# A one-core decoder step: six entries moved in the hand-written order of the recurrence, and one new wait

## What is computed

```
def step(S, inp):
    r_t, w_t, k_t, v_t, kk_t, a_t = inp
    sa = einsum("bhvk,bhk->bhv", S, -kk_t)
    S = S * w_t + sa[..., None] * (kk_t * a_t) + v_t[..., None] * k_t
    o_t = einsum("bhvk,bhk->bhv", S, r_t)
    return S, o_t
...
o = (o - mean) * rsqrt(var + LNX_EPS) * lnx_g + lnx_b
o = o + sum(r * k * r_k) * v
o = o * silu(g)
```

## Time and profile before

| what | value |
|---|---|
| median of three runs | 1921.43 us (1921.3 to 1922.53) |
| the profiled execution | 1924.37 us, span 1922.6 us |
| TensorE busy | 1791.9 us (93%) |
| VectorE busy | 1035.1 us (54%) |
| ScalarE busy | 824.5 us (43%) |
| GpSimd busy | 262.1 us (14%) |
| mean granted TensorE clock | 0.981 |

### The profile page before, as it was taken

One profiled execution on the slowest core, in us unless ns is written; L12 is line 12 of the kernel. 1 busy time (PEld: TensorE's weight loads), 2 busy tenths in 40 slices (PEclk: granted clock), 3 DMA queues, 4 the chain that ended last, 5 costly groups with the idle time before them and its releaser, 6 DMA issues.

```text
span 1922.6 us, 44084 instructions
## 1 busy us (share of the span) xinstructions
PE 1791.9 (93%) x18432; PEld 1521.4 (79%) x18432; DVE 1035.1 (54%) x1654; ACT 824.5 (43%) x1555; POOL 262.1 (14%) x331
## 2 busy tenths in 40 slices
PE   7999999999999999999999999999999998777897
PEld 6988999999888887799987676767776775333697
DVE  6744354463588888245445443444464444676334
ACT  4334233333588887424233332323334444655233
POOL 0300000000256665232000000000000000010132
PEclk9999999999999999999999999999999998999899
DMA  7534544554345653244799999999999999999441
GB/s 280 194 136 171 179 161 166 180 167 160 110 125 153 157 129 96 98 166 166 309 343 420 419 421 396 415 426 426 425 426 404 423 423 375 420 390 363 189 144 71
DMA packets 155929, 510.45 MB, mean 266 GB/s; under 512 B 60289, under 2 KB 82178, under 8 KB 110978
## 3 DMA queue, kind: packets, MB, share of 16 engines
q1 hardware_dynamic: 153442, 503.66, 69.1%
q10 hardware_dynamic: 2304, 4.20, 0.8%
HBM read 472.86 MB, written 32.32 MB: 263 GB/s over the span
## 4 chain that ended last, share of the span: by engine, by line
PE 35%; DMA 15%; DVE 3%; ACT 2%; issue 2%; SPq 1%; DVEq 0%; ACTq 0%
DMA at_vraw<-in_cache_v 15%; PE psP L2673 8%; PE psP L2674 8%; PE psP L2675 8%; PE at_psO L2727 5%; PE at_psS L2706 4%; SPq L2086 0%; PE psP L2772 0%; PE at_psT L2718 0%; SPq L2126 0%; ACT at_p_w L2393 0%; ACT at_p_w L2391 0%; PE psP L2794 0%; DVE at_o_new L2590 0%; DVE at_p_rc L2618 0%
## 5 line engine op out<-in xcount | busy, mean ns | idle before, releaser
L2673 PE MATMUL psP<-xhi,whi 128*128 128x320 f32 x1488 | 475.7, 320 | 2.9 <-DVE xlo L2560 1.9
L2675 PE MATMUL psP<-xhi,wlo 128*128 128x320 f32 x1488 | 460.9, 310 | 0.0
L2674 PE MATMUL psP<-xlo,whi 128*128 128x320 f32 x1488 | 460.6, 310 | 0.0
L2673 PEld LDWEIGHTS psP<-xhi,whi 128*128 128x128 f32 x1488 | 280.5, 188 | 66.7 <-issue 65.2
L2435 DVE TENSOR_TENSOR wlo<-wraw,whi 128x2048 fp32r<-128x2048 f32 x92 | 212.9, 2315 | 204.6 <-ACT whi L2261 204.4
L2261 ACT ACTIVATE whi<-wraw 128x2048 fp32r<-128x2048 f32 x92 | 176.0, 1913 | 278.0 <-PE psP L2675 276.7
L2674 PEld LDWEIGHTS psP<-xlo,whi 128*128 128x128 f32 x1488 | 281.0, 189 | 0.1
L2675 PEld LDWEIGHTS psP<-xhi,wlo 128*128 128x128 f32 x1488 | 280.4, 188 | 0.0
L139 PE MATMUL psP<-xhi,whi 128*128 128x320 f32 x704 | 218.1, 310 | 2.6 <-DVE wlo L174 2.3
L140 PE MATMUL psP<-xlo,whi 128*128 128x320 f32 x704 | 217.5, 309 | 0.0
L141 PE MATMUL psP<-xhi,wlo 128*128 128x320 f32 x704 | 217.5, 309 | 0.0
(11 more groups left out here) (382 smaller groups left out, 3080.0 us busy)
## 6 DMA issues: line engine op xcount, KB each, us to landing
wraw<-in_weights SPq DMA_DIRECT2D x156, 1024.0 KB, 5.9
at_kraw<-in_cache_k SPq DMA_DIRECT2D x96, 1024.0 KB, 10.9
at_vraw<-in_cache_v SPq DMA_DIRECT2D x94, 1024.0 KB, 10.7
at_kraw<-in_cache_k SPq DMA_DIRECT2D x64, 512.0 KB, 9.4
at_vraw<-in_cache_v SPq DMA_DIRECT2D x62, 512.0 KB, 10.6
rw_s0t<-in_s0T SPq DMA_DIRECT2D x16, 256.0 KB, 3.5
o_wkv_s<-rw_SN SPq DMA_DIRECT2D x16, 256.0 KB, 3.4
wraw<-in_weights ACTq DMA_DIRECT2D x16, 256.0 KB, 3.7
```

Of the source, the lines that this page charges most:

```text
L2673: pe.matmul(out, wh, c_.xhi[:, kc, :], start=(kc == 0), stop=False)
L2674: pe.matmul(out, wh, c_.xlo[:, kc, :], start=False, stop=False)
L2675: last = pe.matmul(out, wl, c_.xhi[:, kc, :], start=False, stop=(kc == NM - 1))
```

## The change

Six entries of ORDER get another place, none is added or dropped. On ScalarE, Ht goes ahead of Pc and Q4 ahead of A12. On GpSimd, Vnx goes ahead of Rz. On VectorE, Bz goes from behind Z1 to ahead of it, directly behind ST2, and bonus from ahead of Z1 to behind it. The entry of y moves back in the string, behind O0, which changes its place towards none of GpSimd's other steps; SP's place for the load of g moves with it. And y gets a wait: in slot s it now waits until VectorE has done Bz of the same slot (tile t + 3). The order of TensorE's steps and of SP's transfers is the same as before.

```diff
@@ ORDER
-P.t.s4 F.a.sq P.t.Ht F.v.cs P.t.AB F.a.kk0 P.v.s3 F.a.Pc R.t.U0 P.v.D4s R.t.mean P.v.D P.a.Ht F.a.ka1 P.v.Dt P.t.XB
-R.a.U0 R.v.cen P.t.D2 F.g.k2 P.a.XB P.v.FR R.a.csq R.t.SA0 R.t.Q4 P.g.ID P.v.KK R.a.SA0 P.a.D2 P.a.A12 F.g.csm R.t.S0
-R.a.Q4 R.t.var R.v.ST0 R.t.U4 P.v.D2t R.a.SP1 R.t.U1 R.a.lnv F.v.rk F.t.ss P.t.W R.a.U1 R.a.U4 R.a.rstd P.v.Kt R.t.SA1
+P.t.s4 F.a.sq P.t.Ht F.v.cs P.t.AB F.a.kk0 P.v.s3 P.a.Ht F.a.Pc R.t.U0 P.v.D4s R.t.mean P.v.D F.a.ka1 P.v.Dt P.t.XB
+R.a.U0 R.v.cen P.t.D2 F.g.k2 P.a.XB P.v.FR R.a.csq R.t.SA0 R.t.Q4 P.g.ID P.v.KK R.a.SA0 P.a.D2 R.a.Q4 P.a.A12 F.g.csm
+R.t.S0 R.t.var R.v.ST0 R.t.U4 P.v.D2t R.a.SP1 R.t.U1 R.a.lnv F.v.rk F.t.ss P.t.W R.a.U1 R.a.U4 R.a.rstd P.v.Kt R.t.SA1
 P.t.D4t R.a.SA1 F.v.ssm P.a.Kn R.t.SA4 P.v.W R.t.S1 P.a.D4t R.t.O1 R.a.SA4 R.v.ST1 R.v.on P.t.Y R.g.SAx R.a.O1 F.a.ln
-P.v.Bt R.t.U2 F.g.Rz P.v.Y R.t.O4 F.a.rn F.t.bon R.a.U2 P.v.Yt F.a.Pm R.g.Vnx F.v.kk R.t.SA2 R.a.O4 P.t.E R.a.SA2
-F.v.Az R.a.ong R.t.SN P.a.E R.g.oy F.a.Pi P.v.Et R.a.SP2 R.t.S2 P.a.Bn R.v.SNa F.g.ka P.t.E2t R.v.ST2 P.t.Z1 F.v.bonus
-R.g.y R.a.SP3 R.t.U3 P.a.E2t P.v.Z1 R.t.O0 R.a.U3 R.t.O2 F.v.Bz R.a.O0 F.g.Kz R.t.SA3 R.a.xh P.t.X R.a.SA3 R.a.O2
+P.v.Bt R.t.U2 R.g.Vnx F.g.Rz P.v.Y R.t.O4 F.a.rn F.t.bon R.a.U2 P.v.Yt F.a.Pm F.v.kk R.t.SA2 R.a.O4 P.t.E R.a.SA2
+F.v.Az R.a.ong R.t.SN P.a.E R.g.oy F.a.Pi P.v.Et R.a.SP2 R.t.S2 P.a.Bn R.v.SNa F.g.ka P.t.E2t R.v.ST2 F.v.Bz P.t.Z1
+R.a.SP3 R.t.U3 P.a.E2t P.v.Z1 F.v.bonus R.t.O0 R.a.U3 R.t.O2 R.a.O0 R.g.y F.g.Kz R.t.SA3 R.a.xh P.t.X R.a.SA3 R.a.O2
 R.t.S3 R.g.xl P.v.X R.t.O3 P.v.X1t R.a.O3 R.g.SNb P.v.Vn R.v.ST3
@@ recurrence, GpSimd
                     elif name == "y":
+                        if t + 3 < TILES:
+                            F.v.wait(pool, "Bz", t + 3)
                         R.g.wait(pool, "oy", t)
                         loaded(pool, "g", t)
```

## The result

The changed kernel took 1930.71 us (median of five, 1927.16 to 1934.06) against 1921.43 us before (median of five, 1920.72 to 1923.51). The medians lie 9.3 us apart; the ratio on record is 1.0040, 95% interval 1.0021 to 1.0059: slower, by 4 to 11 us, and outside the range that I had given. The profiled execution took 1928.53 us with a span of 1926.7.

The account below looks back on a forecast made before the run. The recurrence's 15.51 us slot, closed through W, TensorE's run to X and D, was taken as the bound; 1.8 us (eight slots), 0.6 (two) and 0.1 (others) made +2.5, so 1923.9 us, range 1918.0 to 1926.6.

Parts of the forecast that it names:

- What bounds the slot: Recurrence slot of 15.51 us: D2t releases W, TensorE runs to X, then VectorE's X, cumulative sum and next D.
- Ht and Q4 at 0: ScalarE reordering ahead of W: worth 0, hidden by VectorE's queue from D to D2t; uncovered, up to 0.48 us a slot.
- Vnx ahead of Rz, a gain of 0.35 at X: GpSimd: SN no longer waits for Vnx, so TensorE's run to X comes 0.35 us earlier in eight slots.
- B's product undisturbed at 0.48, no gain from it: VectorE, ahead of Z1: product takes 0.48 us instead of 1.00, but X waits for TensorE anyway, so no further gain.
- The late y by way of xh, SA3, S3, at 0.22 a slot: GpSimd's y waits for B's product, delaying xh, SA3's copy, S3 and D: slot 0.22 us longer (0.10 to 0.31).
- The rival, the sum behind SNb: VectorE's cumulative sum falls behind GpSimd's SNb: 0.42 us a slot, +4.0 us in all, 1925.4; chance 0.18.
- TensorE's stalls: Rival: TensorE's issue waits move to other slots, −1 to −3.5 or +1.2 to +2.4 us, 1919 to 1926; chance 0.14.
- The sum: Total over the recurrence's slots: +2.5 us, giving 1923.9 us on the median's scale.
- A slip in the working: Bounds on D's start in the late-y step: 629.20 with handoffs of 0.05, giving the lower 0.10 us a slot.

Follow-up runs that it names:

- e12: Kernel before with only the two ScalarE moves, Ht ahead of Pc and Q4 ahead of A12: slot 15.51 us, as before; ratio 0.9983.
- e5: Kernel before with only Vnx moved ahead of Rz on GpSimd: slot 15.80 us against 15.51; ratio 1.0009.
- e1: Changed kernel with Vnx put back behind Rz on GpSimd: slot 16.01 us against 16.20; ratio 1.0015.
- e9: Kernel before with Rz ahead of SAx, SNb behind the next slot's cumulative sum, Ht ahead of Pc, four PC buffers: slot 15.13 us, ratio 0.9978.
- e10: Kernel before with SNb waiting for the next slot's cumulative sum and four PC buffers instead of three: slot 15.46 us, ratio 0.9992.
- e3: Changed kernel with xh moved behind O2's copy on ScalarE: slot 16.20 us, unchanged; ratio 1.0016.
- e4: Changed kernel with SNb on GpSimd waiting for the next slot's cumulative sum: slot 15.93 us against 16.20; ratio 1.0018.

## Why the prediction was wrong

- *What bounds the slot.* Right up to X, wrong behind it. D2t, W and TensorE's run to X are as I read them, and AB had only some 0.07 us in hand. But I took the sum to follow from X. Its start does; its end lay 0.68 us behind SNb's, in each of the last twelve slots of the kernel before. I had noted that figure among the rivals and didn't use it in the forecast. GpSimd's y, Kz, xl and SNb closed the slot.
- *Ht and Q4 at 0.* Right (e12).
- *Vnx ahead of Rz, a gain of 0.35 at X.* **This is the first step that failed**, in two ways. An earlier X could not bring D forward while SNb held the sum: in e5 X came 0.28 earlier and D didn't. And I looked for Rz's reader and not for what runs on VectorE where Rz would now stand. There it met kk, and ka, y and SNb came 0.30 later. In the changed kernel X came only 0.05 us earlier (from the D before: 12.80 us after 682.53, against 12.85 after 613.59). Alone the move costs 0.29 (e5); in the changed kernel 0.19 (e1). The size itself was right: 0.33 in e9 against e10.
- *B's product undisturbed at 0.48, no gain from it.* Right: a median of 492 ns, and X waits 0.47 us for TensorE instead. With ka late, it ran from 693.64.
- *The late y by way of xh, SA3, S3, at 0.22 a slot.* The waits came, 0.58 us of each in the slot shown; **as the price of the slot this step failed.** Without it the slot is the same (e3). The slot was set by the rival with SNb. The path is only the second longest: with the sum freed it sets the slot, at 15.93 (e4). That is 0.42 above the kernel before, where I had 0.22; part of it belongs to the late ka, and no run separates the two.
- *The rival, the sum behind SNb.* I gave it 0.18 and a toss-up of 0.01 us. It came in every slot from the fifth sum on, and at 0.69 a slot it was dearer than the 0.42 of its price. With Vnx put back, the slot was 0.50 longer (e1); the other 0.19 is kk's. The reason that I had against it, a VectorE step that already waits gets in when GpSimd changes instructions, didn't help: the sum came 0.03 us after SNb's start, with nothing to wait at. I had the two starts 0.01 us apart and they were 0.03 apart, but both about 0.3 later behind D than in my working, so that this closeness is luck. The Trainium skill, SBUF — State Buffer, section "Who interferes with whom", has it that the two engines' shared access is an exclusive lock and that issue order decides who waits. The trace agrees in both places: kk ends 0.35 after Rz, the sum 0.69 after SNb, each somewhat less than its length alone (0.45 and 0.81).
- *TensorE's stalls.* They are there in each version, in other slots; they made no sign of their own.
- *The sum.* +2.5 us forecast; +5.9 in the recurrence by the profile, +7.7 (4.0 to 11.3) by the ratio. That it came out slower, as forecast, doesn't speak for the forecast: the path that I had priced did not set the time. What lies between 5.9 and 7.7 is not settled: e3, with the same slot and 6.0 us in the stretch, has a ratio of 1.0016 (0.9995 to 1.0037), some 3 us, and the rest of the span varied from 1706 to 1719 us over the profiled executions of all versions, without a pattern that I could tie to an edit.
- *A slip in the working.* With handoffs of 0.05 in place of 0.08, three times over, D would come at 629.23 and not at 629.20; the lower bound of 0.10 a slot should have been 0.13. It changes nothing else.

## What to carry to other kernels

Before a gain is followed to the step that closes the slot, ask what that step's predecessor really ends with. Here the sum took 0.98 us where it takes 0.81 alone, and that excess was the sign that its end hung on another engine.

When a GpSimd instruction is moved in time, list the VectorE instructions with two SBUF inputs that run where it lands, and follow the delay through both queues: a meeting cost the one that came second up to 0.56 us (kk) and 0.90 us (the sum) here, and the loser's successors made new meetings. A forecast that hangs on which of two starts comes first by 0.01 us belongs in the range, at full weight, not in a rival. When one wait is taken away, look for what ends next: e4 gave back 0.27 of 0.69. And before a step is made to wait so that it gets out of the way, look whether another order gives the same without a wait: the version with the shortest slot here (e9) does so.

## What the runs showed of the hardware

- A VectorE step with two inputs in SBUF and an elementwise step of GpSimd didn't run side by side; the one that came second took longer. On VectorE: kk 1.01 us for 0.45 behind Rz, B's product 1.14 for 0.48 behind y, the sum 1.71 for 0.81 behind SNb. On GpSimd: Vnx 0.86 for 0.61, oy 1.16 for 0.86, Kz 1.12 for 0.86. Beside GpSimd's steps, the bonus, which has an input from PSUM, kept its 0.48 us beside y, before and after; the transpose behind X kept 0.45 beside xl.
- The end of the step that came second hung on the end of the first, not on its own start. In all 72 slots of before, changed, e1, e3, e5 and e12 from the fifth sum on, the sum started 0.02 to 0.84 us behind SNb's start, took 1.71 down to 0.91 us, and ended 0.68 to 0.69 us behind SNb's end. That is why the slot repeats to 0.02 us although the start of the sum moves.
